# Expert stage of a streaming encoder on one core: the sync engine's wait for the first gathered rows ahead of the weights of slots four and five

## The reference

```python
def hier_moe(h, w_rg, b_rg, w_re, b_re, w_gate, w_up, w_down):
    # top-1 expert group, then top-2 experts inside it
    g_logits = hs @ w_rg + b_rg;  g_sel = argmax(g_logits);  p_g = softmax(g_logits)[g_sel]
    e_in = (hs @ w_re + b_re).reshape(S, 4, 8)[g_sel]
    top_v, top_i = top_k(e_in, 2);  w2 = softmax(top_v) * p_g
    gates = one_hot(g_sel * 8 + top_i, 32) . w2
    a = einsum('sd,edf->sef', hs, w_gate);  b = einsum('sd,edf->sef', hs, w_up)
    act = silu(a) * b * gates
    return einsum('sef,efd->sd', act, w_down)
```

## Time and profile before

| what | us |
|---|---|
| median of 3 runs | 1292.13 |
| lowest, highest | 1291.89, 1296.58 |
| profiled execution, whole | 1292.51 |
| profiled execution, span | 1290.8 |
| TensorE busy in the span | 1179.1 (91%) |
| mean granted TensorE clock | 0.955 of full speed |

### The profile page before, as it was taken

One profiled execution on the slowest core, in us unless ns is written; L12 is line 12 of the kernel. 1 busy time (PEld: TensorE's weight loads), 2 busy tenths in 40 slices (PEclk: granted clock), 3 DMA queues, 4 the chain that ended last, 5 costly groups with the idle time before them and its releaser, 6 DMA issues. The chain is left out here.

```text
span 1290.8 us, 19011 instructions
## 1 busy us (share of the span) xinstructions
PE 1179.1 (91%) x7174; PEld 661.5 (51%) x7175; DVE 672.5 (52%) x1313; ACT 356.4 (28%) x781; POOL 213.3 (17%) x250
## 2 busy tenths in 40 slices
PE   5999999999978997899999999899967999799795
PEld 1455555555544556666777676555544443233231
DVE  0245444554466884467777765555462444344333
ACT  1122222222222444265555453233320000000000
POOL 4000000000000002354433332011112221121101
PEclk9999999999998998799999999899967999899998
DMA  8721221111136871421111005452448999999992
GB/s 360 298 66 34 65 63 35 58 40 54 48 127 230 295 282 40 124 58 30 29 30 30 1 1 166 158 209 94 168 147 313 346 338 380 386 378 384 352 348 51
DMA packets 92834, 213.47 MB, mean 165 GB/s; under 512 B 20673, under 2 KB 54707, under 8 KB 77394
## 3 DMA queue, kind: packets, MB, share of 16 engines
q1 hardware_dynamic: 82258, 195.02, 41.1%
q0 software_dynamic: 7200, 17.33, 5.3%
q10 hardware_dynamic: 3296, 0.02, 0.1%
HBM read 185.03 MB, written 34.13 MB: 170 GB/s over the span
## 5 line engine op out<-in xcount | busy, mean ns | idle before, releaser
L2402 PE MATMUL g_GU<-w_gu,first_region 128*32 128x512 f32 (+2 forms) x672 | 141.0, 607 | 6.6 <-issue 6.6
L1921 PE MATMUL f_C<-first_region,oT 128*128 128x512 f32 x256 | 115.3, 603 | 0.0
L454 PE MATMUL U<-region,b_hT 128*128 128x512 f32 x256 | 112.3, 592 | 0.0
L2610 DVE TENSOR_TENSOR g_sig<-g_GU,g_sig 128x256 f32<-128x256 f32 x23 | 9.8, 425 | 168.8 <-ACT g_sig L2560 168.8
L1723 DVE TENSOR_TENSOR_SCAN region<-region,early 128x128 f32<-128x128 f32 (+7 forms) x64 | 88.7, 1406 | 6.1 <-POOL region L1530 6.1
L2402 PEld LDWEIGHTS g_GU<-w_gu,first_region 128*32 128x32 f32 (+2 forms) x672 | 43.8, 126 | 68.1 <-issue 67.1
L454 PE MATMUL b_UL<-region,b_hT 128*128 128x384 f32 (+1 forms) x256 | 75.3, 453 | 1.8 <-DMA region<-w_in 1.8
L1921 PEld LDWEIGHTS f_C<-first_region,oT 128*128 128x128 f32 x256 | 48.1, 193 | 54.3 <-issue 54.2
L454 PEld LDWEIGHTS U<-region,b_hT 128*128 128x128 f32 x256 | 47.5, 190 | 54.2 <-issue 54.0
L2381 POOL DMA_INDIRECT y<-oT,g_li x23 | 36.4, 1585 | 230.8 <-DVE oT L2628 180.1
L1592 PE MATMUL e_Z<-first_region,region 104*128 104x512 f32 (+3 forms) x192 | 70.5, 505 | 0.3 <-ACT region L1685 0.3
(11 more groups left out here) (489 smaller groups left out, 2146.0 us busy)
## 6 DMA issues: line engine op xcount, KB each, us to landing
w_gu<-w_gate SPq DMA_DIRECT2D x22, 1024.0 KB, 27.5
w_gu<-w_up SPq DMA_DIRECT2D x22, 1024.0 KB, 32.4
w_down<-w_down SPq DMA_DIRECT2D x22, 1024.0 KB, 25.2
region<-w_ada SPq DMA_DIRECT2D x16, 1024.0 KB, 6.3
region<-w_in SPq DMA_DIRECT2D x3, 2048.0 KB, 16.9
oT<-w_gate SPq DMA_DIRECT2D x5, 1024.0 KB
oT<-w_up SPq DMA_DIRECT2D x5, 1024.0 KB
oT<-w_down SPq DMA_DIRECT2D x5, 1024.0 KB
```

What stands on the lines that cost most here:

```text
L454: end = nc.tensor.matmul(dst[0:T, 0:c1 - c0], lhsT=hT[:, k, 0:T], rhs=g.w_in[:, k, c0:c1], start=k == 0, stop=k == KD - 1)
L1921: end = nc.tensor.matmul(C[n % 2][:, c * 512:(c + 1) * 512], lhsT=g.oT[:, i, k, :], rhs=wo[:, k, c * 512:(c + 1) * 512], start=k == 0, sto ...
L2402: end = nc.tensor.matmul(GU[h * n:h * n + n, :], lhsT=xT[:, b, k, h * n:h * n + n], rhs=wgu[s][:, :, k, :], start=k == 0, stop=k == KD - 1 ...
L2610: mark(nc.vector.tensor_tensor(sig[:], GU[:, 0:DE], sig[:], ALU.mult))
```

## The change

One line is taken out of SP's list at the beginning of `phase_g`:

```diff
                 load_down(nc, io, g, sp, expert(p), s, wd_in[s])
 
-            sp.wait_ge(xg_in[0], 16)
             for p in order[FIXED:]:
                 weights(p)
             sp.wait_ge(st_y, 16 * NB)
```

## The result

| | before | changed |
|---|---|---|
| median of 7 runs, us | 1292.95 | 1298.06 |
| lowest, highest | 1291.89, 1296.58 | 1293.60, 1299.45 |
| profiled execution: span, us | 1290.8 | 1297.8 |
| mean granted TensorE clock | 0.955 | 0.952 |

The ratio of the changed kernel to the one before is 1.0030, 95% interval 1.0017 to 1.0043: 3.9 us slower (2.2 to 5.6).

A forecast was written before the change was run, and what follows sets the result against it. The first gather was taken to be on the path that sets the end, with weights bounding only the stage's later part. 4.8 + 0.5 + 0.4 + 0 = +5.7 us on 1292.13 gave 1297.8; 8-in-10 range 1292.5 to 1301.0.

The forecast's parts named there:

- Forecast A: Expert stage's beginning: first gather slowed at head and service, the rest shifts; 1295.5 to 1300 us, chance 0.45.
- SP's early start: Expert stage's beginning: without its 5.7 us wait SP issues weights near 969.4, that much earlier; gain as such 0.
- Term 1: First gather beside the weights: first records come late and service is slower, +4.8 us (bounds 0 and +9.5).
- rival C: First gather: waits one turn of the weights, then is served in one piece, taking under 6 us; chance 0.22.
- Term 2: Second gather: beside weights it follows the first by 4.1 us, so PE waits, +0.5 us (bounds 0 and +2).
- Term 3: Third gather: block 2's list, issued under the weights, takes about 9 us; PE waits +0.4 us (bounds 0 and +4).
- Term 4: PE's later waits for weights: everything shifts equally, the lead does not shorten them, 0 us (bounds 0 and -5.7).
- D: Later weight stream: started earlier it ends earlier, PE's waits shrink; at best 1284.5, likelier 1287 to 1292 us; chance 0.10.

The follow-up runs named there:

- x0: The changed kernel as it is, measured and profiled a second time; ratio to the kernel before 1.0024 (1.0013 to 1.0035).
- x3: Kernel before with five extra clears on POOL ahead of the first gather, SP's wait kept, so gather and weights start later; ratio 1.0030 (1.0016 to 1.0043).
- x1: Kernel before with only the fifth expert's gate matrix (1 MB) issued ahead of SP's wait for the first gather; ratio 1.0006 (0.9995 to 1.0017).
- y3: Kernel before with SP waiting for a semaphore POOL raises behind its first gather, instead of for that gather's landing; ratio 1.0033 (1.0021 to 1.0044).
- y2: Kernel before with SP waiting only until both first gathers are issued, instead of for the first one's landing; ratio 1.0024 (1.0013 to 1.0034).
- y1: Kernel before with SP waiting for the gather of block 2 in place of that of block 0; ratio 1.0033 (1.0022 to 1.0044).
- y0: The kernel before, unchanged, measured and profiled a second time; ratio to itself 0.9999 (0.9989 to 1.0008).
- x2: Kernel before with all three matrices of the fifth expert (3 MB) issued ahead of SP's wait for the first gather; ratio 1.0021 (1.0011 to 1.0032).
- z3: As x1, but without ACT's wait for the first gather, so lists from block 2 on go out early; ratio 1.0000 (0.9986 to 1.0014).

## Why the prediction was right, step by step

It forecast +5.7 us and 1297.8; measured were 1298.06 and a ratio worth 3.9 us (2.2 to 5.6). Forecast A happened; a change within 0.5% was put at 0.58. That the median lies within 0.3 us of the forecast is luck: the repeat x0 had 1296.28, and the ratios give 3.9 and 3.1 us, at and below the low end of A's own range of +3.5 to +7.7.

- *SP's early start.* Right: at +2.59 instead of the +2.24 worked out, 5.3 us early instead of 5.7. The gain of 0 for the early weights was right as far as x3 can tell, about 2 us either way.
- *Term 1, +4.8.* Right: +4.3 and +4.7 in the two profiles. The head cost 2.8 us (2.9 in x0), forecast 3; the service 1.5 us (about 2 in x0), forecast 2. Both parts are seen apart: x1 has a head and next to nothing beside it, y3 has the service and no head.
- *The turn in whole packets (rival C).* Its first half came near: q0's first record stands behind 165 records of q1, some ten on each engine, 2.8 us late where C had 2.3. (C's 0.28 us a record averages 365 records of 8 KB with 46 of 4 B; those of 8 KB take 0.32 us each.) Its second half, service in one piece, did not come. The counts, 94 beside 93 from 977 to 979, don't show that, since nine for nine would give the same. The start times of the single records do: each of the 99 gather records of 4 KB that begin 4.0 to 9.5 us after the issue has a record of q1 that begins 2 to 5 ns before its end, and 60 ns later the same test finds one for 13. An engine here turned to the weights behind every record. Under the Trainium skill (DMA: Bandwidth & Descriptors, Queues, rings and completion order), which has an engine drain a whole packet of about 9 to 17 descriptors from one queue before it turns, a gather's nine records for each engine would have followed one another.
- *Term 2, +0.5.* Right: 3.76 us between the first two turnings instead of 3.39, +0.4.
- *Term 3, +0.4.* Measured 0: the list took 7.7 us from ACT's issue instead of 9, and the third rows were there when PE came. That this list and gather are the next to be late was right, and y2 shows how near it was: there it is the whole loss.
- *Term 4, 0.* Right for this change, by a reason that was half wrong. Right: the stream, ahead of PE, runs dry (share 0.40 from 992 to 994) and starts again at PE's pace; up to the tenth turning each is 4.4 us late. Wrong: that the room of 0.79 at 1044 to 1048 makes the start of the stream worthless in both directions. y1 starts it 7.1 us later and pays 4.3 us. By these runs weights and PE are near balance: making the weights earlier brings nothing, making either late costs. I had weighed only D's direction.
- *The size.* +5.7 was some 2 us too high. One part is the profiled execution that it was worked out from: between the changed kernel's two ends and that execution's are 4.4 and 4.9 us, but only 2.1 and 2.6 us to the second profile of before. Another is that PE's late start does not arrive whole: in x1 1.7 us at the first rows and 2.8 at the third (4.3 against y0) became 0.8 us (-0.6 to 2.2). How much of the 4.4 us is absorbed so in the changed kernel was not measured apart.

## What to carry to other kernels

Where it is as here, a transfer on which the next stage's first work depends should have the DMA engines to itself for its few microseconds; bulk loads issued beside it gain nothing if their consumer comes later, and they can double the small transfer's time (4.4 us became 8.7 to 9.1). Look not only at the first such transfer but at the chain behind it (here list, gather, rows of block 2): a 1 KB load behind 6 MB can hold as much as the gather does. And before calling a start time free, try it in both directions.

## What the runs showed that I had not expected

- Whose records come first decides the head. In the nine profiles in which the weights' first record comes after q0's, that one begins 1.69 to 1.70 us after the gather's issue; in the five in which it comes before (changed, x0, x1, x2, z3), 4.09 to 4.55 us after. In the changed kernel the weights are issued 0.05 us after POOL begins its gather, and still their first record begins at 972.81, 0.7 us ahead of where q0's would have.
- The 1 KB list of block 2 took 3.0 us to POOL's next issue when it went out 1.0 us ahead of the weights and 8.7 us when together with them (before and y2).
- A semaphore that POOL's list raises directly behind an indirect DMA does not mark the end of its issue: in y3 SP's first weights went out 0.82 us after the gather began on POOL (+3.34 against +2.52), although the gather occupies POOL for 1.05 us and SP needs 1.0 us for the expert's number in between.
- The two profiles of the unchanged kernel divide PE's waits for weights quite differently (1.5 and 7.3 us against 3.6 and 4.1) and differ by 2.3 us at the end. A single wait of the later stage is no measure of a change of this size.
